# Hybrid decoder trunk on one Trainium2 core: first weights and x in pieces, idle matmuls first, state updates on more array tiles, a new table of steps

## The chip, the core and the metric

The kernel runs on one core of a Trainium2 chip. The core has a matrix engine (TensorE, PE in the profile, with its weight loads PEld), three other engines (VectorE = DVE, ScalarE = ACT, GpSimd = POOL), a synchronisation engine (SyncE = SP) that here only issues DMAs, and 16 DMA engines behind queues. The engines run their own instruction streams in order and meet at semaphores. The metric is the device time of one execution in microseconds; less is better.

## The reference, cut to what matters

Two layers are applied to 256 prompt rows and 32 sample rows (8 sequences of 4 tokens), of 1024 features:

```python
xn = rmsnorm(x, norm1_g)
z = xn @ w_in + b_in                       # 4368 columns, split for four mixers
o_a = gated linear attention (chunks of 64, a state of 64 x 128 per head, 4 heads)
o_b = gMLP: u * (masked W_s @ layernorm(gelu(v)))
o_c = silu(layernorm(depthwise_conv(c_a * sigmoid(c_g), width 31)))
o_d = sliding-window attention with sinks, softmax over 128 keys and the new ones
x = x + (sum_b sigmoid(xn @ w_gate_b) * (o_b @ w_branch_b)) @ w_out
x = x + (silu(g) * up) @ w_down,  g, up = rmsnorm(x, norm2_g) @ w_gate_up
```

The linear attention's update is what is tiled anew: after a chunk, S = diag(a) S + sum_j k_j^T v_j, once for each of the prompt's four chunks and once for each sample sequence, with S an output. All arithmetic is float32; the weight products are made from two parts of each operand, as the next section says.

## The kernel before

Features lie on the 128 partitions and all T = 288 rows (prompt, then samples) are columns. A weight block is 128 x 1024 numbers (512 KB, eight units of 128 columns), and a layer has 158 blocks: 34 for `z`, 32 for the gates, 16 for the branches, 8 for `w_out`, 44 for gate and up, 24 for down. SP loads blocks into a ring of four slots, `raw`. ACT's `split` (L841) rounds a block to `w_hi`; DVE (L1194) or POOL (L1644) makes the rest, `w_lo` = `raw` - `w_hi`. `LO_ON_VECTOR` says which blocks of the first 70 of a layer DVE takes (0 to 3 and 10 in layer 0); from block 70 it is always DVE. The activations have the same parts, `x_hi` (ACT, L1060) and `x_lo` (DVE, L1209). PE's `split_mm` makes three matmuls for each unit (L418, L419, L423), so 24 for a block, and adds them in one of two PSUM banks (banks 0 and 1, `t % 2`), which must be drained before the next block but one may start. ACT drains most blocks (L846 for z, L852 for gates), DVE the first eight of z (`drain_c`, L1219).

The norm of x is applied late: the first eight z blocks (`C_TILES`, the convolution's inputs) are made of unnormed x and multiplied by `rs` (1/rms) when they are drained; in layer 0 the first two, which end before `rs` is known, are copied by ACT (L1102) and multiplied afterwards (L1216). `rs` comes from squares (L1087), three halving additions on DVE (L1524), a sum over partitions on PE (`sum_of`, L438) and Ln and Exp on ACT (L860, L863). At the eighth block ACT and DVE make the normed x.

Beside the blocks run the mixers, one generator on each engine. After each block PE sets `place` to the block's number in its layer and takes the next part of `mixers`; each part begins with `at(name)`, which lets it start once `place` has reached `STEP[name]`. A part whose number is already passed starts at once behind the one before it, and the order of the parts in an engine's generator is fixed. ACT does the same in its loop: in turn t it drains block t-1, splits block t+3, then takes a part. Numbers 0 to 33 are z blocks, 34 to 65 gates, 66 to 81 branches. DVE has no such numbers for most of its mixers: `CONV_RUNS` says how many steps of the convolution (two instructions, L1271, for one of 62 taps) it makes between two of their parts.

Parts that matter below, with the line numbers of before: `lr_sums` (PE L454, after block 8, waits for the normed x); scores and softmax (DVE L1332, L1311, PE L516, L544); `att_in` (L570, L582, 64x64 tiles of the array); `updates` (PE L605, chunk updates in the halves of the array that take rows 0-63 and 64-127; `state` is written by DVE, L1427 and L1429); `from_state` (L614, needs `state`); `smp_old` (L634, the old states times q) and ACT's `old_out` (L990), which in ACT's generator stands behind `gelu` (L986); `smp_out` (L641); `smp_update` (L677, eight sample updates in two groups, four row tiles, added by DVE at L1470); and `mixed` (L705, L707), the gMLP's product, group by group, two prompt matmuls and then the sample one. A full float32 matmul is two passes in the trace, each an instruction with its own weight load.

At the start SP issues the parameters `prm`, the first half of x and then the weights; ACT issues the other half of x and, behind its first weight split, the constants `cst` (1110 KB), for which the first `sum_of` waits.

## Time and profile before

| | us |
|---|---|
| median of 3 runs | 1116.13 |
| lowest, highest | 1115.69, 1117.11 |
| the profiled execution | 1116.88 |
| its span, first to last instruction | 1115.1 |
| PE busy | 1088.6 (98%) |
| DVE, ACT, POOL busy | 694.1, 594.1, 455.9 |
| PE matmul instructions | 8416 |

The span is measured from the first instruction of the program. A matmul's busy time overlaps the next one's, since the array is a pipeline, so the distance between two starts tells more than a duration; where rows are merged ("x16") the distance from one row's start to the next row's tells it. Idle time in brackets is that of the engine in front of the instruction, with the instruction that ended it.

### The profile page before, as it was taken

What the parts mean: (1) busy time and instruction counts of PE and PEld (TensorE: products, weight loads), DVE (VectorE), ACT (ScalarE), POOL (GpSimd) and SP (SyncE); (2) the same over time, 40 slices, a digit from 0 to 9 for tenths busy, and PEclk for the clock granted to TensorE, in tenths of its full rate; (3) what the DMA queues carried; (4) which work ended last, traced back from release to release, by engine and by line L of the source; (5) the groups of instructions that cost most, each with busy time, mean ns of one, the idle gap of its engine ahead of it and who ended that gap; (6) DMA issues with size and microseconds to landing.
All of it is one profiled execution on the core that took longest, in us unless ns stands there. A gap on an engine that the chain in (4) does not pass through costs nothing.

```text
span 1115.1 us, 20200 instructions
## 1 busy us (share of the span) xinstructions
PE 1088.6 (98%) x8416; PEld 1062.7 (95%) x8416; DVE 694.1 (62%) x1016; ACT 594.1 (53%) x890; POOL 455.9 (41%) x250
## 2 busy tenths in 40 slices
PE   5999999999999999999999999999999999999999
PEld 5999979999999999999999997999999999999998
DVE  7594868650886555565548867785348756556543
ACT  5564664776545544444446557557674554444431
POOL 1688735766352111101167866547735421111000
PEclk9999999999999999999999999999999999999999
DMA  6746443554447576555545455335444555555653
GB/s 248 228 150 207 132 133 96 152 152 137 152 126 263 173 219 186 171 167 167 174 144 164 153 171 168 96 114 152 150 135 150 182 186 180 171 168 151 191 160 91
DMA packets 61483, 181.48 MB, mean 163 GB/s; under 512 B 16048, under 2 KB 18736, under 8 KB 60720
## 3 DMA queue, kind: packets, MB, share of 16 engines
q1 hardware_dynamic: 60816, 176.37, 51.3%
q10 hardware_dynamic: 576, 3.82, 0.9%
q8 instruction: 67, 1.10, 0.4%
q14 instruction: 24, 0.20, 0.1%
HBM read 174.93 MB, written 7.27 MB: 163 GB/s over the span
## 4 chain that ended last, share of the span: by engine, by line
PE 92%; DVE 3%; ACT 3%; issue 1%; DMA 1%; SPq 0%; ACTq 0%; DVEq 0%
PE ps L418 29%; PE ps L423 28%; PE ps L419 28%; DVE work L1311 1%; ACT w_hi L841 1%; DVE qz L1389 1%; PE ps L438 1%; DMA raw<-in_w_z 1%; PE ps L461 0%; PE ps L705 0%; DVE ps L1271 0%; DVE work L1524 0%; PE ps L677 0%; PE ps L605 0%; PE ps L516 0%
## 5 line engine op out<-in xcount | busy, mean ns | idle before, releaser
L418 PE MATMUL ps<-x_hi,w_hi 128*128 128x288 f32 x1952 | 585.3, 300 | 15.3 <-DVE x_lo L1209 10.6
L419 PE MATMUL ps<-x_lo,w_hi 128*128 128x288 f32 x1952 | 577.1, 296 | 0.0
L423 PE MATMUL ps<-x_hi,w_lo 128*128 128x288 f32 x1952 | 575.3, 295 | 0.0
L1644 POOL TENSOR_TENSOR w_lo<-raw,w_hi 128x1024 fp32r<-128x1024 f32 x131 | 340.8, 2618 | 191.4 <-ACT w_hi L841 191.2
L841 ACT ACTIVATE w_hi<-raw 128x1024 fp32r<-128x1024 f32 x316 | 328.0, 1052 | 164.9 <-PE ps L423 141.5
L418 PEld LDWEIGHTS ps<-x_hi,w_hi 128*128 128x128 f32 x1952 | 367.3, 188 | 23.1 <-DVE w_lo L1194 10.6
L423 PEld LDWEIGHTS ps<-x_hi,w_lo 128*128 128x128 f32 x1952 | 368.8, 189 | 0.0
L419 PEld LDWEIGHTS ps<-x_lo,w_hi 128*128 128x128 f32 x1952 | 367.8, 188 | 0.7
L1194 DVE TENSOR_TENSOR w_lo<-raw,w_hi 128x1024 fp32r<-128x1024 f32 x185 | 231.1, 1250 | 127.6 <-ACT w_hi L841 127.6
L1668 POOL TENSOR_TENSOR work<-work,rs 128x288 f32<-128x288 f32 x44 | 35.8, 814 | 237.9 <-ACT work L1155 237.9
L423 PE MATMUL ps<-h_hi,w_lo 128*128 128x288 f32 x352 | 104.4, 296 | 0.0
L418 PE MATMUL ps<-h_hi,w_hi 128*128 128x288 f32 x352 | 104.0, 296 | 0.0
L419 PE MATMUL ps<-h_lo,w_hi 128*128 128x288 f32 x352 | 102.6, 292 | 0.0
L1271 DVE SCALAR_TENSOR_TENSOR ps<-hist_p,prm,ps 128x256 f32<-128x256 f32 x240 | 96.7, 481 | 0.3
L1155 ACT ACTIVATE work<-work 128x288 f32<-128x288 f32 x44 | 19.6, 445 | 107.8 <-DVE work L1609 107.8
L1663 POOL TENSOR_TENSOR zg<-zg 128x288 f32<-128x288 f32 x48 | 51.1, 1088 | 55.5 <-DVE zg L1569 55.3
L419 PEld LDWEIGHTS ps<-h_lo,w_hi 128*128 128x128 f32 x352 | 67.1, 191 | 0.0
L1639 POOL TENSOR_TENSOR work<-work 128x288 f32<-128x288 f32 x21 | 25.5, 1214 | 100.4 <-ACT work L1071 100.4
L418 PEld LDWEIGHTS ps<-h_hi,w_hi 128*128 128x128 f32 x352 | 66.1, 188 | 0.0
L423 PEld LDWEIGHTS ps<-h_hi,w_lo 128*128 128x128 f32 x352 | 66.0, 187 | 0.0
L852 ACT ACTIVATE zg<-ps,prm 128x288 f32<-128x288 f32 x64 | 31.8, 497 | 59.5 <-PE ps L423 59.4
L846 ACT ACTIVATE zg<-ps,prm 128x288 f32<-128x288 f32 x52 | 25.9, 498 | 68.5 <-PE ps L423 68.5
(232 smaller groups left out, 1052.5 us busy)
## 6 DMA issues: line engine op xcount, KB each, us to landing
raw<-in_w_up SPq DMA_DIRECT2D x88, 512.0 KB, 4.1
raw<-in_w_z SPq DMA_DIRECT2D x68, 512.0 KB, 3.8
raw<-in_w_gate SPq DMA_DIRECT2D x64, 512.0 KB, 3.6
raw<-in_w_branch SPq DMA_DIRECT2D x32, 512.0 KB, 3.6
raw<-in_w_down SPq DMA_DIRECT2D x32, 512.0 KB, 3.7
raw<-in_w_out SPq DMA_DIRECT2D x16, 512.0 KB, 3.6
raw<-in_w_down SPq DMA_DIRECT2D x16, 384.0 KB, 3.2
kv<-in_state ACTq DMA_DIRECT2D x2, 1024.0 KB, 7.1
```

The costliest lines, as they stand in the source:

```text
L418: pe.matmul(out, wh, rh, start=start, stop=False)
L419: pe.matmul(out, wh, rl, start=False, stop=False)
L423: return pe.matmul(out, w_lo[:, slot, u * UNIT:(u + 1) * UNIT], rh, start=False, stop=stop)
L841: act.activation(w_hi[:, slot, :], raw[:, slot, :], ACT.Copy).then_inc(hi_done, 1)
L846: ins = act.activation(z[:, t, :], ps[:, t % 2, 0:T], ACT.Identity, bias=p("b_in", t))
L852: act.activation(gate[:, t, :], ps[:, t % 2, 0:T], ACT.Identity, bias=p("b_gate", t)).then_inc(bank_free[t % 2], 1)
L1194: dve.tensor_tensor(w_lo[:, slot, :], raw[:, slot, :], w_hi[:, slot, :].bitcast(f32), ALU.subtract)\
L1271: ins = dve.scalar_tensor_tensor(out=acc, in0=src, scalar=w, in1=acc, op0=ALU.mult, op1=ALU.add)
L1639: pool.tensor_tensor(sq[:, 0, :], sq[:, 0, :], sq[:, k, :], ALU.add).then_inc(squares, 1)
L1644: pool.tensor_tensor(w_lo[:, slot, :], raw[:, slot, :], w_hi[:, slot, :].bitcast(f32), ALU.subtract).then_inc(lo_pool, 1)
L1663: pool.tensor_tensor(gate[:, d, :], gate[:, d, :], gate[:, t, :], ALU.add).then_inc(summed, 1)
L1668: pool.tensor_tensor(gate_s[:, k % 2, :], gate_s[:, k % 2, :], rs[:, :], ALU.mult).then_inc(gate_ready, 1)
```

## The change

Start of the program. The first x is loaded in four pieces of two feature tiles (three on ACT's queue, one on SP's), and the first weight block in two halves on SP's queue in front of its piece of x. ACT and DVE split blocks 0 and 1 by halves of 512 columns, and PE starts a block's first four units when the first half is there. The constants are put in another order and loaded in two parts, `ones` and the two epsilons (130 columns) early, the rest from ACT's turn 6. DVE clears a quarter of `qz` first, and PE makes five float32 matmuls on it (ten passes) before its first weight block; nothing reads what they write. DVE also makes `w_lo` of blocks 4 and 5 of layer 0. Five z tiles (0 to 4) instead of two are drained unscaled by ACT and multiplied later, behind the eighth block and behind the low part of block 10; `c_gate` in layer 0 waits for them, has a step of its own (12) and the first sum of squares and its rsqrt stand one block later.

State updates. `updates` puts each head's 64 x 128 product on one of four 64x64 tiles (row half by column half) with 128 columns, where a pass had 256 columns and half of what it made was unused; `smp_update` does so on eight 32x64 tiles. The products of a state then lie together in PSUM, and DVE copies or adds them in one instruction where it took two or four.

`mixed` makes all eight prompt matmuls, then the four of the samples.

The tables: most numbers of `STEP` are two higher, some one, and `CONV_RUNS` has a row of 27 for each layer. For layer 0 it begins 7, 2, 0, 2, 5, 3, 0, 3, 2, 1, 12 and for layer 1 7, 2, 0, 3, 5, 2, 0, 4, 1, 0, 12, where both had 7, 2, 0, 5, 6, 1, 0, 4, 3, 1, 8. Numbers used below, old to new: scores0 23 to 25, exp_s 31 to 33, v_copied 34 to 39, decay_exp 37 to 38, att_in 38 to 40, chunks 40 to 42, chunk1 41 to 42, gelu 42 to 45, chunk3 (with smp_old behind it) 43 to 45, n1_rstd of layer 1 0 to 1.

```diff
-LO_ON_VECTOR = ((0, 1, 2, 3, 10), (0, 1, 2, 10))
+LO_ON_VECTOR = ((0, 1, 2, 3, 4, 5, 10), (0, 1, 2, 10))
...
-    smp_pv=31, smp_od=34, decay_in=32, decay_log=21, v_copied=34, decay_exp=37, att_in=38, k_copied=32, gelu=42,
-    chunks=40, smp_old=36, old_out=35, smp_out=45, gla_o=38, cv_mean=46, cv_sq=47, smp_update0=52, smp_update1=55,
...
+    chunk1=42, chunk2=43, chunk3=45, gla_spread=51, n1_sums=0, n1_rstd=1, n1_sums0=2, n1_rstd0=3, c_gate0=12,
...
+    v_copied=39, decay_exp=38, att_in=40, k_copied=28, gelu=45, chunks=42, smp_old=33, old_out=40, smp_out=46,
...
+FIRST = SLOT // 2
+UNSCALED = 5
+FIRST_CONSTS = CONST_AT["heads"]
+WARM_UP = 5
+CONSTS_AT = 6
...
+            w0 = row("w_z", 0)
             params(0)
-            sp.dma_start(x[:, 0:KC // 2, :], x_half(0)).then_inc(x_in[0], 16)
+            sp.dma_start(raw[:, 0, 0:FIRST], w0[:, 0:FIRST]).then_inc(raw0_in, 16)
+            sp.dma_start(raw[:, 0, FIRST:SLOT], w0[:, FIRST:SLOT]).then_inc(raw_in[0], 16)
+            sp.dma_start(x[:, 6:8, :], x_piece(3)).then_inc(x_in[3], 16)
...
-                            mm = pe.matmul(ps[:, 4 + odd, k * 256:k * 256 + 256], k_tok[rows, a, k * P:(k + 1) * P],
-                                           v_tok[rows, a, k * 256:k * 256 + 256], start=True, stop=True)
+                            for par in range(2):
+                                o, at_h = slice(64 * par, 64 * par + 64), k * P + 64 * par
+                                h = 2 * k + par
+                                mm = pe.matmul(ps[o, 4 + odd, k * P:(k + 1) * P], k_tok[rows, a, at_h:at_h + 64],
+                                               v_tok[rows, a, h * P:(h + 1) * P], start=True, stop=True)
...
-                            mm = pe.matmul(ps[:, 2 + j, k * 256:k * 256 + 256], k_own[r, i, k * P:(k + 1) * P],
-                                           v_tok_s[r, k * 256:k * 256 + 256], start=True, stop=True)
+                            for par in range(2):
+                                o, at_h = slice(64 * par, 64 * par + 64), k * P + 64 * par
+                                h = 2 * k + par
+                                mm = pe.matmul(ps[o, 2 + j, k * P:(k + 1) * P], k_own[r, i, at_h:at_h + 64],
+                                               v_tok_s[r, h * P:(h + 1) * P], start=True, stop=True)
...
                         pe.matmul(ps[:, 4 + a, g * P:(g + 1) * P], gv_tok[:, a, g * P:(g + 1) * P], w_sp[:, g, :],
                                   start=True, stop=True)
+                for g in range(4):
...
+            pe.wait_ge(E("warm"), 1)
+            for _ in range(WARM_UP):
+                pe.matmul(ps[:, 7, 0:T], qz[:, 0, 0:P], qz[:, 0, :], start=True, stop=True)
...
-                yield from at("c_gate")
+                yield from at("c_gate" if l else "c_gate0")
+                act.wait_ge(E("c_scaled"), UNSCALED)
...
+            for i in range(3):
+                act.dma_start(x[:, 2 * i:2 * i + 2, :], x_piece(i)).then_inc(x_in[i], 16)
...
+            act.wait_ge(raw0_in, 16)
+            act.activation(w_hi[:, 0, 0:FIRST], raw[:, 0, 0:FIRST], ACT.Copy).then_inc(hi_half, 1)
...
+            for i in range(4):
+                if i == 2:
+                    act.wait_ge(raw_in[0], 16)
+                    act.activation(w_hi[:, 0, FIRST:SLOT], raw[:, 0, FIRST:SLOT], ACT.Copy).then_inc(hi_done, 1)
+                    act.dma_start(cst[:, 0:FIRST_CONSTS], dram["consts"][:, 0:FIRST_CONSTS]).then_inc(E("eps_in"), 16)
+                act.wait_ge(x_in[i], 16)
+                for k in range(2 * i, 2 * i + 2):
+                    normed_part(1, k)
+            act.wait_ge(raw_in[1], 16)
+            act.activation(w_hi[:, 1, 0:FIRST], raw[:, 1, 0:FIRST], ACT.Copy).then_inc(hi_half, 1)
+            act.activation(w_hi[:, 1, FIRST:SLOT], raw[:, 1, FIRST:SLOT], ACT.Copy).then_inc(hi_done, 1)
             split(2)
+            wait_block(act, 0, Z0)
+            act.activation(z[:, 0, :], ps[:, 0, 0:T], ACT.Copy).then_inc(bank_free[0], 1)
...
+                    if l == 0 and 2 <= t <= UNSCALED:
+                        wait_block(act, l, Z0 + t - 1)
+                        act.activation(z[:, t - 1, :], ps[:, (t - 1) % 2, 0:T], ACT.Copy).then_inc(bank_free[(t - 1) % 2], 1)
+                    if l == 0 and t == CONSTS_AT:
+                        act.dma_start(cst[:, FIRST_CONSTS:CONSTS], dram["consts"][:, FIRST_CONSTS:CONSTS]).then_inc(const_in, 16)
...
-                    for k in range(2):
-                        for par in range(2):
-                            r = slice(64 * par, 64 * par + 64)
-                            u = ps[r, 4 + ch % 2, k * 256 + par * P:k * 256 + par * P + P]
-                            if ch == 0:
-                                ins = dve.tensor_copy(state[r, k, :], u)
-                            else:
-                                ins = dve.scalar_tensor_tensor(out=state[r, k, :], in0=state[r, k, :],
-                                                               scalar=e_pos[r, k, ch * 64 + 63:ch * 64 + 64], in1=u,
-                                                               op0=ALU.mult, op1=ALU.add)
+                    if ch == 0:
+                        ins = dve.tensor_copy(state[:, :, :].rearrange("p a v -> p (a v)"), ps[:, 4, 0:2 * P])
+                    else:
+                        for k in range(2):
+                            ins = dve.scalar_tensor_tensor(out=state[:, k, :], in0=state[:, k, :],
+                                                           scalar=e_pos[:, k, ch * 64 + 63:ch * 64 + 64],
+                                                           in1=ps[:, 4 + ch % 2, k * P:(k + 1) * P], op0=ALU.mult, op1=ALU.add)
...
-                    for par in range(2):
-                        r = slice(64 * par, 64 * par + 64)
-                        u = ps[r, 2:6, :].rearrange("p b (k n) -> p b k n", k=2)[:, :, :, par * P:par * P + P]
-                        ins = dve.tensor_tensor(s_smp[r, 4 * i:4 * i + 4, :, :], s_smp[r, 4 * i:4 * i + 4, :, :], u, ALU.add)
-                    ins.then_inc(E("smp_added"), 1)
+                    new = s_smp[:, 4 * i:4 * i + 4, :, :].rearrange("p b a v -> p b (a v)")
+                    dve.tensor_tensor(new, new, ps[:, 2:6, 0:2 * P], ALU.add).then_inc(E("smp_added"), 1)
...
+            split_half(0, 0, 1, lo_half)
             for k in range(KC):
-                if k == KC // 2:
-                    dve.wait_ge(x_in[1], 16)
+                if k == 4:
+                    split_half(0, 1, 1, lo_dve)
                 normed_part(k + 1, 1, k)
-            split(1)
+            split_half(1, 0, 2, lo_half)
+            split_half(1, 1, 2, lo_dve)
...
+                order = (0, 1, 2, 3, 4, 5, 6) if l else (5, 6)
+                for i, t in enumerate(order):
+                    if i == (2 if l else 0):
+                        dve.tensor_tensor(sq, x[:, :, :], bcast(rs[:, :], KC), ALU.mult).then_inc(E("x_scaled"), 1)
                     drain_c(l, t)
...
+                if l == 0:
+                    split(10)
+                    for t in range(UNSCALED):
+                        drain_c(l, t)
```

DVE from its first instruction, before: whole blocks, x behind the first one.

```order
L1194 TENSOR_TENSOR w_lo<-raw,w_hi 128x1024 [waits hi_done,zeroed]
L1209 SCALAR_TENSOR_TENSOR x_lo<-x,prm,x_hi 128x288 [waits xh_done,x_in0,prm_in]
L1209 SCALAR_TENSOR_TENSOR x_lo<-x,prm,x_hi 128x288 [waits xh_done] x3
L1209 SCALAR_TENSOR_TENSOR x_lo<-x,prm,x_hi 128x288 [waits xh_done,x_in1]
L1209 SCALAR_TENSOR_TENSOR x_lo<-x,prm,x_hi 128x288 [waits xh_done] x3
L1194 TENSOR_TENSOR w_lo<-raw,w_hi 128x1024 [waits hi_done] x2
L1524 TENSOR_TENSOR work<-work 128x1152 [waits x_sq]
L1524 TENSOR_TENSOR work<-work 128x576 [waits dve_link]
L1524 TENSOR_TENSOR work<-work 128x288 [waits dve_link]
L1194 TENSOR_TENSOR w_lo<-raw,w_hi 128x1024 [waits hi_done]
```

The same place now.

```order
L1552 TENSOR_TENSOR w_lo<-raw,w_hi 128x512 [waits hi_half,zeroed]
L1249 SCALAR_TENSOR_TENSOR x_lo<-x,prm,x_hi 128x288 [waits xh_done] x4
L1552 TENSOR_TENSOR w_lo<-raw,w_hi 128x512 [waits hi_done]
L1249 SCALAR_TENSOR_TENSOR x_lo<-x,prm,x_hi 128x288 [waits xh_done] x4
L1552 TENSOR_TENSOR w_lo<-raw,w_hi 128x512 [waits hi_half]
L1552 TENSOR_TENSOR w_lo<-raw,w_hi 128x512 [waits hi_done]
L1234 TENSOR_TENSOR w_lo<-raw,w_hi 128x1024 [waits hi_done]
L1565 TENSOR_TENSOR work<-work 128x1152 [waits x_sq]
L1234 TENSOR_TENSOR w_lo<-raw,w_hi 128x1024 [waits hi_done,dve_link]
L1565 TENSOR_TENSOR work<-work 128x576
L1565 TENSOR_TENSOR work<-work 128x288 [waits dve_link]
L1234 TENSOR_TENSOR w_lo<-raw,w_hi 128x1024 [waits hi_done] x2
```

The halves stand around x_lo, the low part of block 3 between the additions, those of 4 and 5 behind them.

PE in layer 0 at `chunks`, before: a weight block (L418, L419, L423) stands behind the update.

```order
L596 MATMUL ps<-attz,zg 128x128 [waits k_copied,att_done]
L596 MATMUL ps<-attz,zg 128x128 x7
L605 MATMUL ps<-zg,work 128x256 x4
L418 MATMUL ps<-x_hi,w_hi 128x288 [waits bank_free1,lo_pool]
L419 MATMUL ps<-x_lo,w_hi 128x288
```

The same place now.

```order
L610 MATMUL ps<-attz,zg 128x128 [waits k_copied,att_done]
L610 MATMUL ps<-attz,zg 128x128 x7
L622 MATMUL ps<-zg,work 64x128 x8
L631 MATMUL ps<-qz,state 128x2x64 [waits state_step]
L631 MATMUL ps<-qz,state 128x2x64
L431 MATMUL ps<-x_hi,w_hi 128x288 [waits bank_free1,lo_pool]
```

`from_state` of the second chunk (L631) now stands directly behind the update, with its wait for `state`.

ACT in layer 0 around k_copied, now (L881 drains a block, L870 splits one); before, L1001 and L1002 (then L970, L971) stood three turns earlier.

```order
L870 ACTIVATE w_hi<-raw 128x1024 [waits blocks_done,raw_in2]
L1001 ACTIVATE zg<-ps 128x1024 [waits v_turned]
L1002 ACTIVATE work<-ps 128x512
L1005 ACTIVATE work<-work 128x576 [waits decay_sum]
L1006 ACTIVATE work<-work 128x576
L1008 ACTIVATE work<-work 128x576 [waits last_diff]
```

The copies of the turned v stand directly in front of the three exponentials that k waits for.

## Rows read from the trace of the kernel before

**Rows 1.** Page, parts 1 and 4, then PE's waits: total us, times, longest.
```profile
PE 1088.6 (98%) x8416; PEld 1062.7 (95%) x8416; DVE 694.1 (62%) x1016; ACT 594.1 (53%) x890; POOL 455.9 (41%) x250
...
PE ps L418 <- DVE x_lo L1209: 10.6, 1, 10.6
```

**Rows 2.** DMA issues, 0 to 2 us, then 7.7 to 7.9: KB, us to landing.
```profile
raw<-in_w_z SPq DMA_DIRECT2D x1, 512.0 KB, 6.0
prm<-in_params SPq DMA_DIRECT2D x1, 125.0 KB, 3.8
...
cst<-in_consts ACTq DMA_DIRECT2D x1, 1110.0 KB, 6.6
```

**Rows 3.** Timeline, ACT and DVE, 7 to 13 us: start, us, instruction, [idle before].
```profile
7.62 1.06 ACT L841 ACTIVATE w_hi<-raw 128x1024 fp32r<-128x1024 f32 x1 [5.15 <-DMA raw<-in_w_z]
...
8.58 3.50 ACT L1060 ACTIVATE x_hi<-x,prm 128x288 fp32r<-128x288 f32 x8
8.79 1.23 DVE L1194 TENSOR_TENSOR w_lo<-raw,w_hi 128x1024 fp32r<-128x1024 f32 x1 [5.24 <-ACT w_hi L841]
9.93 3.52 DVE L1209 SCALAR_TENSOR_TENSOR x_lo<-x,prm,x_hi 128x288 fp32r<-128x288 f32 x8
```

**Rows 4.** Windows: length, busy by engine (instructions), granted PE clock, DMA share, GB/s.
```profile
10.50:14.00 3.50, 3.41 (x14) 3.44 (x15) 3.50 (x8) 3.50 (x7) 0.00 (x0) 1.00 1.01 401
...
21.00:24.30 3.30, 3.30 (x13) 3.08 (x14) 3.04 (x2) 2.23 (x3) 1.94 (x1) 0.53 0.00 0
...
400.00:432.00 32.00, 32.00 (x242) 32.00 (x242) 18.19 (x26) 13.95 (x20) 4.07 (x5) 1.00 0.70 220
```

**Rows 5.** Timeline, 13 to 46 us: squares, first addition, sum over partitions, lr_sums.
```profile
13.88 2.12 ACT L1087 ACTIVATE work<-x 128x2304 f32<-128x2304 f32 x1
...
16.04 1.36 DVE L1524 TENSOR_TENSOR work<-work 128x1152 f32<-128x1152 f32 x1 [0.32 <-ACT work L1087]
...
20.88 1.02 PE L438 MATMUL ps<-work,cst 128*128 128x288 f32 x2 [1.98 <-DVE work L1524]
...
45.64 0.69 PE L454 MATMUL ps<-work,w_lr 128*32 128x288 f32 x8
```

**Rows 6.** Timeline, PE's small matmuls and what follows `mixed`; DVE's state copy.
```profile
175.58 1.14 PE L605 MATMUL ps<-zg,work 64*128 64x256 f32 x8
...
176.76 0.28 DVE L1427 COPY state<-ps 64x128 f32<-64x128 f32 x1 [1.63 <-PE ps L605]
...
189.01 1.97 PE L634 MATMUL ps<-kv,work 128*64 128x128 f32 x32
...
165.69 0.69 PE L582 MATMUL ps<-qz,work 64*64 64x64 f32 x32
...
225.03 1.15 PE L677 MATMUL ps<-work 32*128 32x256 f32 x16
...
198.40 1.07 PE L641 MATMUL ps<-work 32*128 32x32 f32 x8
...
836.60 0.61 PE L705 MATMUL ps<-w_sp,work 128*128 128x128 f32 x4
...
840.39 0.40 PE L418 MATMUL ps<-x_hi,w_hi 128*128 128x288 f32 x1
```

**Rows 7.** Timeline, 137 to 192 us: PE's waits in layer 0's mix, ACT's late drain.
```profile
137.22 4.79 DVE L1271 SCALAR_TENSOR_TENSOR ps<-hist_p,prm,ps 128x256 f32<-128x256 f32 x12
137.35 1.97 PE L516 MATMUL ps<-cst,work 128*128 128x128 f32 x16 [0.76 <-DVE work L1311]
...
191.02 0.28 ACT L990 ACTIVATE work<-ps 128x128 f32<-128x128 f32 x1 [5.90 <-PE ps L634]
...
191.84 0.37 PE L418 MATMUL ps<-x_hi,w_hi 128*128 128x288 f32 x1 [0.86 <-ACT zg L852]
```

**Rows 8.** Timeline, DVE in layer 0: the wait for the first scores.
```profile
99.52 1.23 DVE L1332 SCALAR_TENSOR_TENSOR work<-ps,cst 128x1024 f32<-128x1024 f32 x1 [10.68 <-PE ps L473]
```

**Rows 9.** Timeline, start of layer 1: DVE's first drain, behind ACT's rsqrt.
```profile
570.40 0.46 DVE L1219 TENSOR_TENSOR zg<-ps,rs 128x288 f32<-128x288 f32 x1 [4.44 <-ACT rs L863]
```

90 lines of the change are left out of this document (46 added, 44 removed).

## The prediction

> **What bounds the kernel now.** I read the page's busy times first: TensorE (PE) works for 1088.6 of 1115.1 us [rows 1], so nearly every microsecond to be had is PE idle, PE at the lower clock, or PE work that could be issued more densely. Then the waits by engine for PE, and the start at close range. The bulk is the weight blocks, 24 matmuls each. From 400 to 432 us there are 242 of them in 32.00 us at full granted clock, 0.132 us each, so a block is 3.2 us [rows 4]. The rest of the program hangs on this pace, and no edit touches it.
>
> The start: the table of landings [rows 2] gives 3.8 us from issue to landing for prm, which goes first, and 6.0 for the first 512 KB of weights, which go behind it and half of x. ACT starts only then, at 7.62 (w_hi, 1.06 us), makes eight x_hi in 3.50 (0.44 each), DVE follows with w_lo (1.23) and eight x_lo in 3.52 [rows 3]; PE's first weight matmul is 10.6 us in [rows 1]. The first 14 matmuls take 3.41 us, 0.24 each: half clock, 1.2 GHz, after idling; later rows run at 0.13 [rows 4]. After two blocks PE waits 1.98 us for the sum of squares (DVE's additions, the first at 16.04); it comes back at the lower clock (granted 0.53 in 21.0 to 24.3, 13 matmuls) [rows 4, 5]. The small lr matmuls, after nine blocks and the sum, start at 45.64 [rows 5]. That instant is my yardstick for the start.
>
> In the mix, one execution of it per layer, PE waits in a few places: 0.76 us for DVE's softmax product, 0.86 us for a bank that ACT drains late [rows 7], and some others.
>
> **The start, part by part.** Bytes moved in front of the first weights don't change (1.83 MB with the first block; about 400 GB/s once they flow [rows 4]). What changes is the order in which they land: prm and the first quarter of x are 0.42 MB; with the first half block and the second quarter, 0.98 MB; with the second half block and third quarter, 1.54 MB. All 1.83 MB land at 7.6 us as before, so going back at 0.4 MB/us the three groups are there at about 4.1, 5.5 and 6.9. ACT then: half w_hi 0.55 from 5.5, x_hi 0 to 3 at 0.44 until 7.8, second half 0.55 until 8.35, x_hi 4 to 7 until 10.2. DVE: w_lo half (0.62) until 6.7, x_lo 0 to 3 until 8.4, half until 9.0, x_lo 4 to 7 until 10.8. PE's first real matmul is at 7.3, not 10.6. The first block is then paced by x_lo (three matmuls per 0.44) if PE has its full clock: it ends at 11.3, the second at 14.7, the third at 17.9. If the clock is low through all of it, it ends 1.2 to 1.7 later.
>
> The sum of squares: ACT reaches Square (2.12 [rows 5]) at about 12.8, once block 0's bank is copied. DVE's first addition took 1.36 for 1152 columns [rows 5]; the others are half and a quarter as wide, so I take 1.36, 0.75 and 0.4, and one w_lo (1.23) put between them: ready at about 18.6. (Before, they ended only at PE's 20.88: 4.8 in all.) PE waits 0.7 us instead of 1.98, then six blocks (19.2) and the sum (0.5): lr_sums at 38.3. With half clock in the first block, that wait disappears and about 39.3 comes out. Against 45.64: 6.3 to 7.5 earlier. I take **-7.0**; bounds -4.5 (pieces land as late as whole loads, idle matmuls bring nothing) and -8.
>
> Idle matmuls cost nothing: from about 1.2 to 6.0 us at 0.48 per pass (twice 0.24) they fill time in which PE has no data. Whether the clock stays up in the 1.3 us behind them I can't see. PE fell to 0.53 after working 18.0 to 18.9 and resting 1.98 [rows 4, 5]; here the rest is shorter.
>
> The five unscaled drains put copies of 288 columns on ACT, about as long as an x_hi (0.44), whose rsqrt now falls a block later, and as many such multiplies on DVE after the eighth block (0.46, as L1219 [rows 9]). Nobody waits for those before c_gate. In layer 0 c_gate goes from step 8 to 12, and so the convolution begins four blocks (12.8 us) later against the blocks. Its readers are mostly two blocks (6.4 us) later, so DVE is 6.4 us in arrears; its 10.68 us gap in front of the first scores [rows 8] swallows that. The constants now go out in the seventh block and need, as before, some 6.6 us beside weight loads [rows 2]: from 28.6 (behind block 8's split) to 35.2, against 38.3. Cost nothing, or up to 3 if they are late.
>
> **The tiled updates.** `updates` now: eight passes of 256 columns in 1.14 us with the tail [rows 6]. New: 16 passes of 128 columns on four tiles. L634 has two column tiles of 128 columns, 32 passes in 1.97, so 0.055 each and a tail of 0.2; on four tiles, 0.027. That makes 0.43 instead of some 0.9: -0.43, four times, **-1.7**. `smp_update`: 16 passes in 1.15 (L677). New: 32 passes on eight tiles, a form that no row has. Bounds: 0.0134 (half of 0.027) and 0.022, the pace of L582 on 64x64 tiles, 32 passes in 0.69 [rows 6]: 0.43 to 0.69 and a tail. I take **-1.0** for four calls (0 to -1.6).
>
> L582 speaks against a rule. The Trainium skill, "TensorE: Matmul & The Clock Gate", section "Wait — 56ns, not 53.3ns?", says that starts never come closer than about 25 ns however short a matmul is. By it, as an estimate, 32 passes would need 0.8 us, the sample updates would gain nothing, and the forecast would be 1 us higher. The row of L582 has 22 ns with its tail, so this trace does not agree.
>
> `mixed`: 3.79 us from 836.60 to 840.39, sixteen prompt passes with two sample passes of another tile shape behind every fourth [rows 6]. Grouped: 16 prompt passes as L516's (16 in 1.97 [rows 7]) and eight like L641's (1.07 [rows 6]), less the tail of the first, with one return: 3.2. Twice -0.6, **-1.2**; bounds -0.4 and -2.5.
>
> **The new table.** ACT's table moves gelu from step 42 to 45. Before, ACT did gelu and then sat 5.90 us until smp_old (L990), which PE issues after the block of step 43; so the bank of block 42 was drained only behind it, and PE lost 0.86 [rows 7]. Now ACT waits in step 45 for smp_old after block 45. The bank missing then is that of block 45, and PE wants it only at 47. The wait goes: 1.0 with the restart, twice, **-2.0**. Next late is nothing nearer than a block. The softmax product: one convolution step less in front of it in layer 0, two less in layer 1 (0.78 each, from twelve in 4.79 [rows 7]). ACT's exp ends at the same place, so of the 0.76 twice I take **-1.0** (0 to -1.5).
>
> Against that: chunks and chunk1 are now both step 42. PE issues the update and at once wants the state, which DVE copies after it (0.28 for 128 columns [rows 6], some 0.4 for 256), where a block stood between. PE waits 0.6 us, behind it the block; twice, **+1.2** (DVE must be standing ready; if it is in a convolution step, up to +2.5). In layer 1 ACT's rsqrt comes after one more w_hi (1.05): DVE's first drain starts at 571.0 instead of 570.40 (the wait for the table load overlaps in part) and ends at 571.5, and PE's third block, due at about 571.1, loses **+0.4** [rows 9]. v_copied now stands ahead of decay_exp (1.5 us on ACT), but DVE's product there was waiting for POOL anyway, so I count nothing (bound +3 for both layers). The other waits of the mix keep their neighbours, two blocks later.
>
> **Sum.** -7.0 -1.7 -1.0 -1.2 -2.0 -1.0 +1.2 +0.4 = -12.3. Span 1115.1 to 1102.8. The profiled execution took 1116.88, 1.8 more than its span and 0.75 over the median; 1116.13 - 12.3 = **1103.8**.
>
> **Rivals.**
> (a) The start gains little. The pieces wait for each other so that ACT's chain still begins near 7 us, and PE's idle matmuls don't hold the clock. For it: both queues share the same engines, and the fall behind the 1.98 us wait. Against: bytes ahead of the first half block are halved. Gain 3, so 1107.8. Chance 0.13.
> (b) New waits in the mix. The v_copied bound (+3), constants late (+1 to 3), a state copy queued behind convolution: together +5, 1109. Against: DVE's 10.68 us gap. Chance 0.12.
> (c) The table removes more than I followed, from the 0.7 to 1.5 us PE waits that I left standing in each layer: -5, 1099. Chance 0.10.
> (d) Slower: the narrow tiles don't overlap. Then each pass lasts its 0.107 (two times 0.0535, twice the column pair's pace): per layer 32 update passes 3.4 instead of 1.7, 64 sample passes 6.8 instead of 1.65, so +13.8 for both layers in place of -2.7. 1103.8 + 16.5 = 1120. It decides from about 12 us of lost overlap. For it: no row has 32x64. Against: 64x64 runs at 0.022 per pass of 64 columns, four row tiles at under 0.07 per pass of 256 [rows 6]. Chance 0.03.
> (e) The idle matmuls don't do what they are for: half clock through the first blocks. That costs 1 us, 1104.8, and lies in the forecast's own range.
>
> **How the numbers follow.** Forecast with (e): 0.62; (a) 0.13, (b) 0.12, (c) 0.10, (d) 0.03. About 0.2% (2 us) is what a measurement of this kernel tells from no change; all but (d) lie far below. Range: from 1099.8, most of (c) left out, to 1109, with (a) and the middle of (b). Faster 0.95, same 0.02, slower 0.03.
>
> **What would show it.** In the new profile: first weight matmul at 7.3 (6.8 to 8.5), with matmuls 0.13 apart soon; lr_sums at 38.3 (38 to 40); the wait for the squares under 1 us; the update passes 0.65 us to the next block, the sample ones 0.7 to 0.9; `mixed` 3.2; no PE wait for a bank behind smp_old; a new 0.6 us PE wait on the state copy, twice. I'm wrong if lr_sums comes after 41, if PE waits for the constants there, or if a wait of over 1 us stands in the mix that the old trace has not.

## The result, and the profile after

The changed kernel takes **1102.87 us** (median; 1102.62 to 1103.15), the kernel before 1116.02 beside it: ratio 0.9879, 95% interval 0.9864 to 0.9895. The forecast was 1103.8, with a range of 1099.8 to 1109.0. The profiled execution took 1103.15, its span is 1101.3, against 1116.88 and 1115.1 before. So the trace shows 13.8 us less and the medians 13.15: the profiled execution of before lay 0.86 over its median, that of after 0.28.

Page of the changed kernel: span, then busy time of each engine.

```profile
span 1101.3 us, 20408 instructions
...
PE 1086.2 (99%) x8522; PEld 1061.0 (96%) x8522; DVE 685.4 (62%) x999; ACT 595.5 (54%) x895; POOL 450.5 (41%) x248
```

That line answers to the first of [rows 1]: PE is as busy as before (5.2 us of it are the idle matmuls), and idle for 15.1 us of the span instead of 26.5. PE's waits, longest sum first (columns: who waits for whom, us in total, times, longest):

```profile
PE ps L567 <- ACT zg L986: 2.4, 2, 1.2
PE ps L431 <- ACT zg L875: 1.7, 4, 0.6
PE ps L584 <- DVE zg L1436: 1.5, 2, 0.7
PE ps L431 <- DVE x_lo L1249: 1.3, 1, 1.3
...
PE ps L631 <- DVE state L1464: 1.1, 2, 0.5
PE ps L530 <- ACT work L971: 0.5, 2, 0.2
PE ps L431 <- DVE zg L1260: 0.4, 1, 0.4
```

The 10.6 us in front of the first x_lo [rows 1] have become 1.3 behind the idle matmuls. Two rows are new: PE behind the state copy, twice, and behind layer 1's first drain (L1260).

**The start.** Landings of what was issued in the first 2 us (KB, median us to landing), then ACT and DVE (start, us, instruction, [idle before]):

```profile
x<-in_x ACTq DMA_DIRECT2D x3, 288.0 KB, 4.6
raw<-in_w_z SPq DMA_DIRECT2D x2, 256.0 KB, 4.9
prm<-in_params SPq DMA_DIRECT2D x1, 125.0 KB, 3.4
```

```profile
5.68 0.63 ACT L1109 ACTIVATE w_hi<-raw 128x512 fp32r<-128x512 f32 x1 [2.25 <-DMA raw<-in_w_z]
...
6.41 0.69 DVE L1552 TENSOR_TENSOR w_lo<-raw,w_hi 128x512 fp32r<-128x512 f32 x1 [2.86 <-ACT w_hi L1109]
7.02 1.80 DVE L1249 SCALAR_TENSOR_TENSOR x_lo<-x,prm,x_hi 128x288 fp32r<-128x288 f32 x4
...
14.96 1.36 DVE L1565 TENSOR_TENSOR work<-work 128x1152 f32<-128x1152 f32 x1 [1.48 <-ACT work L1125]
16.36 1.23 DVE L1234 TENSOR_TENSOR w_lo<-raw,w_hi 128x1024 fp32r<-128x1024 f32 x1
17.50 1.24 DVE L1565 TENSOR_TENSOR work<-work 128x576 f32<-128x576 f32 x2
```

```profile
1.22 5.17 PE L734 MATMUL ps<-qz 128*128 128x288 f32 x10 [1.22 <-DVE qz L1543]
...
7.68 0.58 PE L431 MATMUL ps<-x_hi,w_hi 128*128 128x288 f32 x1 [1.29 <-DVE x_lo L1249]
8.06 0.44 PE L432 MATMUL ps<-x_lo,w_hi 128*128 128x288 f32 x1
...
18.89 0.72 PE L451 MATMUL ps<-work,cst 128*128 128x288 f32 x2
...
38.74 1.18 PE L468 MATMUL ps<-work,w_lr 128*32 128x288 f32 x16
```

ACT begins at 5.68 instead of 7.62 [rows 3], the additions end at 18.75, and PE, busy until 18.86, takes them without a wait. The lr matmuls stand at 38.74, against 45.64 [rows 5].

**The mix.** The tiled updates, the rows of smp_update, the mixing of layer 0, and ACT around smp_old:

```profile
174.55 0.67 PE L622 MATMUL ps<-zg,work 64*64 64x128 f32 x16
...
175.28 0.43 DVE L1464 COPY state<-ps 128x256 f32<-128x256 f32 x1 [0.53 <-PE ps L622]
...
175.76 0.71 PE L631 MATMUL ps<-qz,state 128*128 128x128 f32 x4 [0.55 <-DVE state L1464]
...
219.42 0.69 PE L697 MATMUL ps<-work 32*64 32x128 f32 x32
...
272.45 1.95 PE L725 MATMUL ps<-w_sp,work 128*128 128x128 f32 x16
274.33 1.07 PE L728 MATMUL ps<-w_bd,work 32*128 32x32 f32 x8
```

```profile
187.96 1.15 ACT L1018 ACTIVATE zg<-zg 128x1152 f32<-128x1152 f32 x1
189.67 0.28 ACT L1021 ACTIVATE work<-ps 128x128 f32<-128x128 f32 x1 [0.57 <-PE ps L651]
```

ACT now waits 0.57 us for smp_old, not 5.90 [rows 7].

How I compare the two traces: between two neighbouring weight matmuls I take the start-to-start time less 0.133, the ordinary pace. What is left is what the small matmuls in between and the waits cost there. Summed by place:

| place | before | after | difference, both layers | forecast |
|---|---|---|---|---|
| start, to lr_sums | 45.64 | 38.74 | -6.9 | -7.0 |
| softmax stretch | 12.46 | 11.95 | -1.0 | -1.0 |
| chunks to second update, with the wait for state | 4.92 | 4.72 | -0.4 | -1.7 + 1.2 |
| last chunk, smp_old, bank behind it | 3.36 | 2.43 | -1.9 | -2.0 |
| two sample updates | 2 x 1.17 | 2 x 0.71 | -1.8 | -1.0 |
| mixing | 3.79 | 2.88 | -1.8 | -1.2 |
| convolution's mean (L451) | 0.51 | 0.27 | -0.5 | none |
| layer 1's third block (rsqrt) | 0 | 0.58 | +0.6 | +0.4 |
| sum | | | -13.7 | -12.3 |

### The profile page after: what moved, and what is told of

Its sections match the earlier page's. It is cut to its first block, busy times and chain, and to the rows that moved or that the text cites. A ratio compares the mean times of both kernels' runs of the same rounds, so it can differ in the third digit from the quotient of the medians.

```text
span 1101.3 us, 20408 instructions
## 1 busy us (share of the span) xinstructions
PE 1086.2 (99%) x8522; PEld 1061.0 (96%) x8522; DVE 685.4 (62%) x999; ACT 595.5 (54%) x895; POOL 450.5 (41%) x248
## 4 chain that ended last, share of the span: by engine, by line
PE 93%; ACT 4%; DVE 1%; issue 1%; DMA 0%; SPq 0%; DVEq 0%; ACTq 0%
PE ps L431 30%; PE ps L436 29%; PE ps L432 29%; ACT work L960 1%; ACT w_hi L870 1%; PE ps L451 0%; PE ps L475 0%; DMA raw<-in_w_z 0%; PE ps L509 0%; ACT L884 0%; PE ps L651 0%; DVE qz L1430 0%; PE ps L631 0%; PE ps L610 0%; PE ps L725 0%
## 5 line engine op out<-in xcount | busy, mean ns | idle before, releaser
L1694 POOL TENSOR_TENSOR w_lo<-raw,w_hi 128x1024 fp32r<-128x1024 f32 x129 | 334.1, 2603 | 186.7 <-ACT w_hi L870 186.4
L870 ACT ACTIVATE w_hi<-raw 128x1024 fp32r<-128x1024 f32 x314 | 325.8, 1052 | 152.6 <-PE ps L436 137.8
L881 ACT ACTIVATE zg<-ps,prm 128x288 f32<-128x288 f32 x64 | 31.8, 497 | 66.4 <-PE ps L436 66.1
```

The source lines that it names most:

```text
L870: act.activation(w_hi[:, slot, :], raw[:, slot, :], ACT.Copy).then_inc(hi_done, 1)
L881: act.activation(gate[:, t, :], ps[:, t % 2, 0:T], ACT.Identity, bias=p("b_gate", t)).then_inc(bank_free[t % 2], 1)
L1694: pool.tensor_tensor(w_lo[:, slot, :], raw[:, slot, :], w_hi[:, slot, :].bitcast(f32), ALU.subtract).then_inc(lo_pool, 1)
```

## Experiments

All are the changed kernel with one thing altered. "Block n starts" is worked out from the weight matmuls. Differences are taken against the 1102.87 us above unless the text says "beside it". The kernel before took 1116.02 us then; beside the four on the start (none and six idle matmuls, whole loads, two tiles scaled late) it took 1115.93, beside the next four (both updates wide, four passes in a row, mixing in turn, the old table) 1116.95, and beside the rest 1116.34. So a few tenths, and up to 0.9 us in that second group, belong to the time of measuring; the block starts in the traces are free of that.

**Without the idle matmuls.**

```
-WARM_UP = 5
+WARM_UP = 0
```

> The changed kernel without its five idle matmuls ahead of the first weights. In the trace of the changed kernel they run from 1.2 to 6.4 us, PE then rests 1.3 us, and the first 12 weight matmuls are 0.24 us apart, the rest 0.13; before, without idle matmuls, the first 14 were 0.24 apart. Theory (the idle matmuls bring next to nothing, since PE rests again behind them): 14 slow matmuls instead of 12, +0.2 us at the end of the third block, lr_sums 38.74 to 38.9, total +0 to +0.3 us. Rival (they halve the slow stretch): 24 or more slow matmuls, +1.3 us at the end of the third block, lr_sums 40, total +1.3 us.

Measured: 1103.97 us (1103.41 to 1104.15), 1.1 over the changed kernel and 1.0 over the next experiment's, beside it. The first **19** weight matmuls are 0.24 apart, the second block starts at 13.17 instead of 12.30, lr_sums at 39.59. It lies between the two theories. DVE's first addition moves too, from 14.96 to 15.83: ACT copies block 0's bank before it squares, so the slow block delays the squares as well as PE.

**Six idle matmuls.**

```
-WARM_UP = 5
+WARM_UP = 6
```

> The changed kernel with six idle matmuls instead of five: they end about 1 us later, near 7.4 us, just in front of the first weight matmul at 7.68, so PE hardly rests. Theory A (the rest of 1.3 us is what left the first weight matmuls at the low clock): the first block runs at 0.13 apart from its start and is paced by x_lo, block 3's end comes 1.2 us earlier, but the sum of squares is ready at 18.75 as now, so PE waits about 1.2 us there and lr_sums stays at 38.7 (total -0.2 to +0.2), or, if PE falls to the low clock behind that wait as it did before the change, lr_sums 40 and total +1.4. Theory B (the rest is not the cause): the first 12 weight matmuls stay 0.24 apart and nothing moves, total within 0.2 us.

Measured: 1102.96 us (1102.86 to 1103.18), no difference. Its start is a different one, though: from the second weight matmul on they are 0.13 apart, PE then waits for x_lo in mid-block, and lr_sums are at 38.35. PE did not wait 1.2 us for the squares as I had expected: the first addition came earlier (14.59), through the same coupling.

**The changed kernel again,** with three others (below).

> The changed kernel itself, beside the other three on the same chip. Total 1102.9 within 0.5. The question is its start: theory (how many of the first weight matmuls are slow is not set by the kernel, since kernels with the same start differ): four slow ones and lr_sums near 38.3 as often as not; rival (the twelve of the first trace belong to this kernel): twelve again and lr_sums 38.7.

Measured: 1103.34 us (1102.81 to 1103.99), span 1101.1, lr_sums at 38.41: the theory holds. The same code that had 12 slow weight matmuls now has none. (Only the first distance is longer, 0.20: that stands behind every rest, also at 10.07 to 10.28 in the middle of the fast stretch. At the low clock it is 0.38, 7.68 to 8.06 in the changed kernel's first trace. The "four" of the expectations counts such places of a fast start, so it stands for none.) A window of two starts (length, busy by engine with instructions): first this kernel, then the one without idle matmuls; the timeline of this kernel's first matmuls stands last.

```profile
7.70:9.80 2.10, 1.86 (x12) 1.66 (x12) 2.10 (x5) 2.10 (x6) 0.00 (x0) 1.00 1.03 419
```

```profile
7.70:9.80 2.10, 2.03 (x8) 2.06 (x9) 2.10 (x5) 2.10 (x5) 0.00 (x0) 1.00 1.03 419
```

```profile
7.75 0.37 PE L431 MATMUL ps<-x_hi,w_hi 128*128 128x288 f32 x1 [1.57 <-DVE x_lo L1249]
7.95 0.30 PE L432 MATMUL ps<-x_lo,w_hi 128*128 128x288 f32 x1
...
9.31 0.29 PE L436 MATMUL ps<-x_hi,w_lo 128*128 128x288 f32 x1
10.07 0.37 PE L431 MATMUL ps<-x_hi,w_hi 128*128 128x288 f32 x1 [0.46 <-DVE x_lo L1249]
```

In that stretch twelve matmuls against eight, and the twelve include a wait for x_lo. (The clock column says 1.00 in both; ahead of a trace's first recorded change of the clock it tells nothing, and the distances, 0.24 or 0.13, tell the level.) Over all profiled starts with pieces:

| start | idle passes end | rest | slow weight matmuls | block 1 starts | lr_sums |
|---|---|---|---|---|---|
| no idle matmuls | | | 19 | 13.17 | 39.59 |
| five: changed kernel | 6.38 | 1.3 | 12 | 12.30 | 38.74 |
| five: two others | 5.3, 5.5 | 2.7, 2.2 | 11, 14 | 12.55, 12.49 | 38.99, 38.92 |
| five: six others | 5.98 to 6.39 | 1.1 to 1.7 | 0 | 11.61 to 12.18 | 38.15 to 38.71 (five of them) |
| six: two | 6.50, 7.26 | 1.2, 0.6 | 0 | 11.80, 12.00 | 38.35, 38.52 |

(The sixth of the six others is the kernel with two unscaled tiles, whose lr_sums are late for its own reason.) In the two rows of 5.3 and 5.5 the clock had risen while the idle matmuls ran (the last passes 0.24 apart) and was low again when the weights came, or fell behind the first of them. In the one of 5.3 (three entries moved, below) the granted clock is 1.00 from 4.1 to 7.4 us and from 10.9 to 14.0, and between them 0.50:

```profile
7.50:10.80 3.30, 2.80 (x12) 2.83 (x13) 3.30 (x8) 3.30 (x8) 0.00 (x0) 0.50 1.03 420
```

The rest is longer in these two because passes at the full clock end sooner, so the table doesn't tell whether the length of the rest or the moment at which the clock rose decides; no run set them apart. The Trainium skill, "TensorE: Matmul & The Clock Gate", section "What's actually happening", says that the number of slow matmuls at a kernel's start differs from run to run of one kernel; the 12 and none of one code agree.

**Whole loads.** x in halves, the first weights in one load, issued as before.

```
-            sp.dma_start(raw[:, 0, 0:FIRST], w0[:, 0:FIRST]).then_inc(raw0_in, 16)
-            sp.dma_start(raw[:, 0, FIRST:SLOT], w0[:, FIRST:SLOT]).then_inc(raw_in[0], 16)
-            sp.dma_start(x[:, 6:8, :], x_piece(3)).then_inc(x_in[3], 16)
+            sp.dma_start(x[:, 0:4, :], x_half(0)).then_inc(x_in[0], 16)
+            sp.dma_start(raw[:, 0, :], w0).then_inc(raw_in[0], 16)
...
-            for i in range(3):
-                act.dma_start(x[:, 2 * i:2 * i + 2, :], x_piece(i)).then_inc(x_in[i], 16)
+            act.dma_start(x[:, 4:8, :], x_half(1)).then_inc(x_in[2], 16)
```

> The changed kernel with x in two loads and the first weight block in one, in the order that they had before (parameters, x first half, weights, x second half); the rest of the start as in the changed kernel. Theory (the pieces bring the first weight matmul forward, and the later scaling brings the rest): the weights land at 7.6 us, ACT's first half w_hi at 7.6, first weight matmul 9.4 instead of 7.68, squares ready at 20.4 instead of 18.75, lr_sums 40.5, total +1.8 us (1.3 to 2.5). Rival (a) of the prediction (the pieces wait for each other and gain little): first weight matmul within 0.5 us of 7.68 and total within 0.5 us.

Measured: 1106.10 us (1105.39 to 1106.54), +3.2. Its timeline:

```profile
7.89 0.63 ACT L1107 ACTIVATE w_hi<-raw 128x512 fp32r<-128x512 f32 x1 [5.42 <-DMA raw<-in_w_z]
...
9.90 0.58 PE L430 MATMUL ps<-x_hi,w_hi 128*128 128x288 f32 x1 [4.43 <-DVE x_lo L1247]
```

Rival (a) falls: ACT waits 2.2 us longer for weights, and PE begins 2.2 later. The other 0.8 to 1.2 is the clock: with a rest of 4.43 us behind the idle matmuls all of the first 19 weight matmuls are slow, as without any. lr_sums: 41.72, +3.0. I had left that out of the expectation.

**Two tiles scaled late, the sum one block earlier.**

```
-UNSCALED = 5
+UNSCALED = 2
-    n1_sums0=2, n1_rstd0=3
+    n1_sums0=1, n1_rstd0=2
-                order = (0, 1, 2, 3, 4, 5, 6) if l else (5, 6)
+                order = (0, 1, 2, 3, 4, 5, 6) if l else (2, 3, 4, 5, 6)
```

> The changed kernel with two z tiles scaled late instead of five, and the sum of squares asked for behind the second block instead of the third (the order of before), pieces and idle matmuls kept. Theory (most of the start's gain is that the wait for the squares is covered by one more block): PE ends its second block at 15.5, the additions end at 18.75, so PE waits 3.2 us and comes back at the low clock (+1.4), lr_sums 42 to 43.4, total +3.2 to +4.6 us. Rival (the sum's place does not matter, because the additions come earlier as well): wait under 1 us, lr_sums within 0.7 of 38.7, total within 0.7.

Measured: 1109.41 us (1107.83 to 1109.83), +6.5; the profiled execution is the fastest of these, +4.7 on the changed kernel's.

```profile
18.70 0.72 PE L451 MATMUL ps<-work,cst 128*128 128x288 f32 x2 [3.25 <-DVE work L1565]
```

The wait is the 3.25 of the theory, and behind it the granted clock is 0.66 from 19.0 to 22.3; lr_sums 43.26 instead of 38.7 (+4.5). The other executions are 1.4 to 2.0 slower than the profiled one, and their mean granted clock is 0.995 where it has 0.998: worked out from that, they spent some 7 us more at the low clock. Where, no trace shows. So the start's 6.9 us are: pieces about 2, idle matmuls about 1, and more than half the later sum. The parts don't add up exactly, since each sets how long the next one waits.

**Both updates wide again.** PE's matmuls and DVE's reads of them, as before the change.

```
-                            for par in range(2):
-                                o, at_h = slice(64 * par, 64 * par + 64), k * P + 64 * par
-                                h = 2 * k + par
-                                mm = pe.matmul(ps[o, 4 + odd, k * P:(k + 1) * P], k_tok[rows, a, at_h:at_h + 64],
-                                               v_tok[rows, a, h * P:(h + 1) * P], start=True, stop=True)
+                            mm = pe.matmul(ps[:, 4 + odd, k * 256:k * 256 + 256], k_tok[rows, a, k * P:(k + 1) * P],
+                                           v_tok[rows, a, k * 256:k * 256 + 256], start=True, stop=True)
...
```

> The changed kernel with both state updates as they were: passes of 256 columns on two and four tiles, and DVE's reads of them in halves of the partitions. Between the two traces the stretch of chunks to chunk2 fell by 0.20 us a layer although a wait of 0.6 was added, and each sample update from 1.17 to 0.71 us (beyond the weight matmuls around it). Theory (the pace of the narrow passes is what was gained: 0.43 us for each of four prompt updates and 0.46 for each of four sample updates): +3.6 us, and with DVE's state copy in four parts behind the first update (PE waits for it) up to +4.8. Rival 1, the size in the prediction: +2.7. Rival 2 (the time went elsewhere in the mix, the tiles are worth little): under +1.5.

Measured: 1108.18 us (1107.87 to 1108.39), **+5.3**. By blocks: the second prompt update +0.47, each sample update +0.46, the first prompt update +1.22. That last one is 0.46 for the passes and 0.75 for DVE:

```profile
175.70 1.20 DVE L1462 COPY state<-ps 64x128 f32<-64x128 f32 x4 [0.97 <-PE ps L619]
...
176.96 0.71 PE L628 MATMUL ps<-qz,state 128*128 128x128 f32 x4 [1.30 <-DVE state L1462]
```

Four copies in 1.20 stand where one takes 0.43. With the new place of chunk1, right behind the update, the single copy is worth 0.75 us a layer, where the narrow passes of both prompt updates bring 0.93.

**Four passes in a row on one tile.** Loops in another order, k innermost; the sample update likewise.

```
-                    for k in range(2):
-                        for odd in range(2):
-                            rows = slice(64 * odd, 64 * odd + 64)
-                            for par in range(2):
+                    for odd in range(2):
+                        rows = slice(64 * odd, 64 * odd + 64)
+                        for par in range(2):
+                            for k in range(2):
```

> The changed kernel with the narrow passes in another order: both key groups of one tile in a row, so that four passes in a row go to the same tile where two do now (the same passes and results). Now the passes start 0.0137 us apart on eight tiles and 0.0265 on four, as if each lasted 0.11 and all tiles ran at once. Theory A (every tile has its own turn, the order in which they are issued does not count): each sample update stays at 0.71 us, total within 0.3. Theory B (passes are issued in order and a pass that waits for its tile holds those behind it): a run of four holds the queue for 0.3 us, each sample update takes 1.7 to 2.7 us and each prompt update 0.8 to 1.3, total +6 to +11 us.

Measured: 1103.38 us (1103.18 to 1103.69), +0.5; span +0.4. The sample update:

```profile
219.41 0.74 PE L697 MATMUL ps<-work 32*64 32x128 f32 x32
```

0.74 instead of 0.69 (0.76 instead of 0.71 to the next block). Theory A: each tile works off its own passes, and the order hardly counts. Taken one by one from the traces, the starts show it: in the changed kernel eight of them lie 0.007 us apart, as for one on each tile, and the next eight begin 0.109 after the first eight did, the time of one pass; with four passes in a row for each tile the eight lie 0.013 to 0.014 apart, and each tile's next start still comes 0.109 later (behind the very first pass of a tile 0.16 in both). So eight tiles give half the mean distance of four: 0.0137 us per pass of 128 columns against 0.0265.

**Mixing in turn.**

```
-                for g in range(4):
                     mm = pe.matmul(ps[:, 7, g * TS:g * TS + TS], ...
```

(the second loop's head taken out, so that the sample pass stands in the first loop)

> The changed kernel with the sample passes of the mixing back behind every fourth prompt pass. The stretch took 3.79 us beyond its neighbours before and 2.88 after. Theory (each change of tile shape costs PE about 0.1 us in both directions, and six of the eight changes are gone): the stretch takes 3.79 again in both layers, +1.8 us in all. Rival (part of the fall comes from the later place in the program, with other work beside it): 3.3 to 3.5, +0.8 to +1.2 us.

Measured: 1104.78 us (1104.48 to 1105.64), +1.9; the stretch 3.80 in both layers. The theory holds to 0.01, and the later place has no part in it. Its rows:

```profile
271.87 0.61 PE L725 MATMUL ps<-w_sp,work 128*128 128x128 f32 x4
272.41 0.40 PE L727 MATMUL ps<-w_bd,work 32*128 32x32 f32 x2
272.74 0.71 PE L725 MATMUL ps<-w_sp,work 128*128 128x128 f32 x4
```

From the start of one pair to the next four: 0.33. Sixteen prompt passes in a row took 1.88 and the eight sample passes 1.00, together 2.88; in turn they take 3.80, so six changes of shape cost 0.92, 0.15 each.

**gelu one step earlier.**

```
-    gelu=45
+    gelu=44
```

> The changed kernel with gelu one step earlier on ACT (44 instead of 45), the distance to smp_old that the kernel before had. Theory (the bank wait behind smp_old is set by this one entry): ACT waits for smp_old one block earlier, drains the block behind it late, and PE's 0.93 us come back in each layer: +1.9 us, 1104.8. Rival (the wait went because everything around it was moved): under +0.5.

Measured: 1105.01 us (1104.74 to 1105.25), +1.7 on the changed kernel beside it; +0.93 at block 46 in both layers. The old picture is back:

```profile
189.87 0.28 ACT L1021 ACTIVATE work<-ps 128x128 f32<-128x128 f32 x1 [5.00 <-PE ps L651]
```

```profile
190.68 0.37 PE L431 MATMUL ps<-x_hi,w_hi 128*128 128x288 f32 x1 [0.86 <-ACT zg L881]
```

**The old table on the changed start.** STEP and CONV_RUNS as before, but with n1_sums0=2, n1_rstd0=3, c_gate0=12.

```
-    lr_sums=8, c_gate=9, qk_sq=14, qk_sums=14, qk_rstd=2, qk_turned=26, scores0=25, ...
+    lr_sums=8, c_gate=8, qk_sq=14, qk_sums=14, qk_rstd=5, qk_turned=20, scores0=23, ...
```

> The changed kernel with the table of steps and the convolution's runs of before, but with the changed start's entries (sum behind the third block, c_gate of layer 0 at 12) and both new update forms. By the comparison of the two traces: bank wait behind smp_old back, +0.93 a layer; softmax product +0.51; the sum at 202.78 +0.24; the wait for rsqrt in layer 1 gone, -0.58; the wait for the state copy gone, -0.6 a layer. Theory: +1.6 us in all (1 to 2.2). Rival (the table was remade because the changed start makes the old one late in layer 0: convolution behind its readers): waits of several us in layer 0, +4 us or more.

Measured: 1110.80 us (1109.17 to 1110.95), **+7.9**. The rival was right, in one place of layer 0:

```profile
90.88 3.69 DVE L1368 TENSOR_TENSOR zg<-zg,work 128x1440 f32<-128x1440 f32 x1
```

```profile
94.62 0.69 PE L479 MATMUL ps<-cst,zg 128*128 128x128 f32 x2 [3.97 <-DVE zg L1368]
```

```profile
94.70:99.00 4.30, 4.30 (x28) 3.38 (x28) 4.30 (x11) 0.00 (x0) 2.08 (x1) 0.50 0.72 276
```

PE asks for q and k in their rotated form at 90.6, about 7 us earlier than before, while DVE began its share four blocks later; PE waits 4.0, then works at half the clock (0.50). By block starts that place costs 7.2 us. Everything else in the old table costs 0.7: bank +1.9, softmax +1.0, state wait -1.5, rsqrt -0.6. So most of what the new table does is to keep the start's gain; its own gain is under 1 us.

**Three entries moved.**

```
-    chunk1=42, chunk2=43, chunk3=45, gla_spread=51, n1_sums=0, n1_rstd=1,
+    chunk1=43, chunk2=44, chunk3=45, gla_spread=51, n1_sums=0, n1_rstd=0,
```

> The changed kernel with three entries of the table moved: the two waits of PE for the state (chunk1, chunk2) one block later, so that a block again stands between the first update and the product that reads it, and layer 1's rsqrt one turn earlier (n1_rstd 0). Theory (the waits are where the trace of the changed kernel shows them: 0.81 behind each layer's first update, 0.58 at layer 1's third block, and nothing else is late then): the stretch of chunks falls by 0.73 us a layer, the third block's wait goes, -2.0 us in all, 1100.9. Rival (the next thing is late within the same block, a bank or the sample product): -0.6 or less.

Measured: 1101.80 us (1101.16 to 1101.91), **-1.5** on the changed kernel beside it (1103.34), ratio to before 0.9869 (0.9853 to 0.9886). By blocks -0.69 in layer 0, -0.59 at layer 1's third block, -0.69 + 0.15 there later: -1.8. The row "PE ps L631 <- DVE state" is gone from PE's waits. The 0.15 is the convolution's mean, which PE asks for sooner in layer 1.

**With six idle matmuls as well.**

```
-WARM_UP = 5
+WARM_UP = 6
```

> The three moved entries and six idle matmuls in one kernel. Seven profiled starts so far with idle matmuls and the changed order: four slow weight matmuls in five of them, twelve in one (five idle ones), four with six idle ones. Theory: -2.0 us from the entries and 0 to -0.4 from the start, 1100.6 to 1100.9. Rival (the extra idle matmul delays the first weights): +0.2 against the kernel with the three entries alone.

Measured: **1101.14 us** (1101.05 to 1101.21), ratio to before 0.9865 (0.9850 to 0.9880), 2.2 under the changed kernel beside it and 0.7 under the three entries alone. Of the 0.7, 0.5 stands in the start (lr_sums 38.52 against 38.99), where the one has no slow weight matmul and the other 11. Whether the sixth idle matmul makes the fast start more likely, two starts with it don't tell. It is the fastest of the kernels here.

## Why the prediction was right, point by point

None of its three signs of being wrong is in the trace: lr_sums are at 38.7, no wait for the constants stands there, and PE's longest wait in the mix, 1.2 us (L567), was there before (L553).

**The start** (-7.0; measured -6.9, or -7.2 in the second trace). Two details missed. The pieces landed as worked out (prm and the first quarter of x at 4.2 and 4.4, half blocks at 5.7 and 6.9), but the first weight matmul came at 7.7, not 7.3, since DVE's w_lo half ended 0.4 later. And I let the wait for the squares take up part of a slow first block (1.2 to 1.7 late, 1.0 at lr_sums). It takes up next to nothing, since the squares wait for block 0: all slow against all fast is 13.17 against 11.80 at the second block and 39.59 against 38.35 at lr_sums. (e)'s price of 1 us was about right (1.1 in the medians), its reason incomplete.

One term of the start came true without a reason given. I priced the last addition of the squares at 0.4. It took 2.51 before:

```profile
18.22 2.51 DVE L1524 TENSOR_TENSOR work<-work 128x288 f32<-128x288 f32 x1
```

POOL's first w_lo ran beside it, from 17.97. Now it takes 0.46, since POOL's first w_lo stands at 20.33, behind the additions: blocks 4 and 5 went to DVE. I had not followed that, so this part, about 2 us of the squares' chain, was luck.

**The late drains and constants.** The constants' second part landed at 34.85 (35.2 forecast; issued 1.4 earlier and 1.0 longer under way than I had it), 3.9 us before PE's lr matmuls: free. The five multiplies were not 0.46 each. The timeline has

```profile
38.97 8.64 DVE L1256 TENSOR_TENSOR zg<-zg,rs 128x288 f32<-128x288 f32 x5
```

two of 0.46 and three of 2.52 to 2.54, each of the three ending 0.3 us behind the end of POOL's w_lo beside it. The cover I had named took it: DVE's gap before the first scores fell from 10.68 [rows 8] to 2.41, by 8.3 where I had 6.4.

```profile
99.01 1.23 DVE L1373 SCALAR_TENSOR_TENSOR work<-ps,cst 128x1024 f32<-128x1024 f32 x1 [2.41 <-PE ps L487]
```

The old table shows what the cover hid: with the readers at their old steps, 7.2 us. That was rival (b)'s kind of event, avoided by a margin of 2.4 us.

**Updates** (-1.7, and +1.2 for the state behind them). The old table with narrow passes gives the two apart: 3.99 for this stretch, so the tiles bring 0.93 a layer (forecast 0.86) and the wait costs 0.73 (0.6). Right. DVE's single copy in place of four, which the price took for granted at 0.4, is worth 0.75 a layer.

**Sample updates** (-1.0, bounds 0 to -1.6; measured -1.84). The step that failed in size: no row had eight tiles, and I took a value between the scaled bound 0.0134 and L582's 0.022 [rows 6] and added a tail. It was 0.0137 a pass, the bound itself, and the tail was no longer than that of the wide form. The 0.022 was also misread: 0.69 / 32 has the last pass's tail in it, and I added a tail again. L582's starts are 0.0154 apart, for 64 columns; as neighbour for 128 columns on more tiles, halving the four-tile row was the better one. The rule of the Trainium skill by which starts keep some 25 ns apart ("TensorE: Matmul & The Clock Gate", section "Wait — 56ns, not 53.3ns?") does not hold in this row either: 13.7 ns in the mean, 7 ns from tile to tile.

**mixed** (-1.2; measured -1.82). The group of sixteen took 1.88, not 1.97, and the group of eight 1.00. The busy times of single rows contain their tails, and I took off one of two. In its bounds of -0.4 to -2.5.

**Bank and softmax** (-2.0, -1.0; measured -1.9, -1.0). Right, and the first is one entry's doing. **rsqrt** +0.4; measured +0.58. **v_copied** ahead of decay_exp: priced at nothing; PE's wait for L1436's product stands unchanged (0.7 us, twice). **Not seen:** 0.24 a layer at the convolution's mean, where DVE's sum used to end just behind PE's last weight matmul.

**Rival (d)** is refuted by the wide form, 5.3 us slower; (a) by whole loads. (c)'s cause, waits removed that I had left standing, did not come: they are in the table of waits as before. The surplus came from terms that I had in the sum, sample updates and mixed, and from the convolution's mean. Of the 1.5 us by which the trace fell further than forecast, 0.6 is the profiled executions' place beside their medians, and the time came out at 1102.87 against 1103.8.

## What to carry to other kernels

A start that is moved forward moves every request behind it; price the table of later steps against the earlier clock of requests, not against the old trace, and look for the helper engine whose chain did not move with them. Small matmuls on disjoint tiles of TensorE overlap fully here, in both orders tried, while each change of tile shape costs about 0.15 us: narrow them, and group them by shape. Where two engines hand a small result to and fro, let a block stand between; two table entries were worth 0.7 us a layer here, the narrowed prompt update 0.9.

## What the runs showed of the hardware

- Eight tiles of 32 x 64: a pass of 128 columns every 0.0137 us in the mean; four of 64 x 64: 0.0265; two of 128 x 64: 0.0547. With four passes in a row on the same tile 0.05 us more per 32.
- The count of slow weight matmuls at the start, with one and the same code: 12 and none. With idle matmuls and a rest of up to 1.7 us behind them eight starts of nine had none, with a rest of 2.2 and 2.7 there were 14 and 11, with 4.4 there were 19, as many as without idle matmuls. A fast first block is worth some 1.2 us.
- DVE's multiply of two SBUF operands: 0.46 us, or 2.52 while POOL's w_lo ran. The last addition of the squares shows the same, 2.51 and 0.46. The Trainium skill, "SBUF — State Buffer", section "SBUF: two separate sides", has DVE and GpSimd exclude each other for whole instructions at a shared port pair, among others where DVE reads two SBUF inputs; the rows agree. Part of the earlier squares is owed to blocks 4 and 5, whose low parts went from POOL to DVE; that part was not measured apart.
